# Three scatter blocks of 3, 3 and 2 chunks in the expert stage of a decoder trunk, the third one after the transposes

## The chip, the cores and the metric

One core of one Trainium2 chip runs the whole program. The metric is the device time of one execution in microseconds, lower is better; the time before is the median of three runs.

## The reference, cut to what matters

The reference is a two-layer decoder trunk over 512 tokens of width 1024. Each layer adds a mixer (a convolution in layer 0, a gated linear attention in layer 1), a cross-attention over 256 memory tokens, and a mixture of experts. The change lies in the mixture of experts, which picks two of 32 experts for every token:

```python
def hier_moe(h, w_grp, b_grp, w_exp, b_exp, w_gate, w_up, w_down):
...
    def expert_block(args):
        xb, e = args
        return (jax.nn.silu(xb @ w_gate[e]) * (xb @ w_up[e])) @ w_down[e]
...
    y = y_buf[dest] * g_flat[order][:, None].astype(h.dtype)
    out = jnp.zeros((T, D), h.dtype).at[token_idx].add(y)
```

Each expert has three matrices, of 1024x512, 1024x512 and 512x1024 float32, 2 MB each. They are read from memory once per layer, 12.58 MB for two experts.

## The kernel before, in words

The kernel is written engine by engine: one function for each engine, whose instructions run in the order in which they stand, with semaphores between them. The residual stream lies as `xT`, eight chunks of 128 features by 512 tokens. The experts of a layer are taken in 16 pairs (`p`, `NP = 16`), and two pairs make a quad (`q`). Nothing is indexed: tokens are gathered and scattered by products with one-hot matrices.

TensorE's list for pair `p` (`moe_segment` of the tensor block) is, before the change:

- `gates(p)` (L668), four small products with the gate table;
- `up(p, 0)` (L628), the gate matrices of both experts, 32 matmul records;
- `scatter(p, range(0, 4))` (L681), chunks 0 to 3 of the output of the pair before: for each chunk a product of `yhi` and one of `ylo` with `onehotT`, 512 columns, into one bank; then VectorE adds the bank to `xT` (`accumulate`, L1728);
- `up(p, 1)` (L628), the up matrices;
- `scatter(p, range(4, 8))`, chunks 4 to 7;
- `transposed(p)` (L688), four transposes of `hidden`, which VectorE makes (L1749) from the results of the two `up`; ScalarE copies them to `hidT` (L1324);
- one `gather` of two chunks for the next quad (L698), which ScalarE copies to `xg`; the last two pairs of a layer have none, since no quad is left;
- `down(p)` (L656), the down matrices, which need `hidT`; then ScalarE makes `yhi` (L1330) and VectorE `ylo` (L1755);
- a second `gather` (L698) and `one_hot_T(p)` (L707). The last pair of a layer has its down product in two halves (`down_half`, L642).

Gates, chunks, gathers and the one-hot transpose share three banks of PSUM (5, 6 and 7). `unit(r, p, k)` gives the place of each use in one sequence: `k` is 0 for the gates, 1 to 8 for the chunks 0 to 7, 9 and 10 for the gathers, 11 for the one-hot transpose. Use `n` goes to bank `n % 3`, and it waits until use `n - 3` has been read (`x_read0` to `x_read2`), by VectorE where that was a chunk, by ScalarE where it was a gather or the one-hot transpose. `x_full0` to `x_full2` say that a use has been written. `taken(p, k)` waits until a certain use has been read.

The weights come through SyncE's DMA queue into `ring`, six slots of 2 MB, exactly one pair. Each half slot (1 MB) is loaded again when the product that read it is done (`pair_loads`, L1049): the gate and up matrices by halves, the four halves of the down matrices together after `down`.

After the last pair `scatter(NP, range(0, C))` brings its eight chunks in one block.

Of the kernel before, what the change touches and what calls it, by code (L numbers as in the profile page):

```python
# [107 lines left out]
def build(nc, a, out):  # L108
# [3 lines left out]
    n = 0  # L112
# [9 lines left out]
    with ExitStack() as ctx:  # L122
# [111 lines left out]
        def bank(b, lo=0, hi=BANK):  # L234
            return PS[:, b * BANK + lo:b * BANK + hi]
# [104 lines left out]
        def unit(r, p, k):  # L340

            if p == -1:
                n = k - 8
            elif p == 0:
                n = 4 if k == 0 else k - 4
            elif p < NP - 2:
                n = 12 * p - 4 + k
            elif p == NP - 2:  # L350
                n = 12 * p - 4 + min(k, 9)
            else:
                n = 12 * p - 6 + min(k, 9) if p < NP else 12 * p - 9 + k
            return n % 3, PER_ROUND * r + n // 3
# [27 lines left out]
        def _(pe):  # L382
# [217 lines left out]
            def moe_segment(l, r):  # L600
# [3 lines left out]
                def use(p, k):  # L604
                    b, n = unit(r, p, k)
                    if not main or n:
                        pe.wait_ge(g[f"x_read{b}"], n)
                    return XBANK + b, g[f"x_full{b}"]

                def taken(p, k):  # L610
                    b, n = unit(r, p, k)
                    pe.wait_ge(g[f"x_read{b}"], n + 1)
# [59 lines left out]
                def scatter(p, cs):  # L672
                    if cs[0] == 0:
                        pe.wait_ge(g["ylo_done"], YS * r + p)
                        taken(p - 1, 11)
                    for c in cs:
                        if p == NP and c == C // 2:
                            pe.wait_ge(g["ylo_done"], YS * r + NP + 1)
                        b, done = use(p, 1 + c)
                        for w in (yhi, ylo):  # L680
                            mm = pe.matmul(bank(b), w[:, c * P:(c + 1) * P], onehotT[:, :],  # L681
                                           start=(w is yhi), stop=(w is ylo))
                        mm.then_inc(done, 1)
# [31 lines left out]
                for p in range(NP):  # L715
                    q, s = p // 2, p % 2
                    more = q + 1 < NQ
                    gates(p)
                    if s == 0:
                        for k in ((8, 9, 10, 11) if p == 0 else (9, 10)):  # L720
                            taken(p - 1, k)
                        if p >= 2:
                            for k in (9, 10):
                                taken(p - 2, k)
                    up(p, 0, "gate_full")
                    if p:
                        scatter(p, range(0, 4))
                    up(p, 1, "up_full")
                    if p:
                        scatter(p, range(4, 8))  # L730
                    transposed(p)
                    if more:
                        if s == 0:
                            pe.wait_ge(g["onehot_ready"], HOTS * r + q + 1 + TT)
                        gather(q + 1, p, 9, 4 * s)
                    if p < NP - 1:
                        down(p)
                        if more:
                            gather(q + 1, p, 10, 4 * s + 2)
                        one_hot_T(p)  # L740
                    else:
                        down_half(p, 0)
                        one_hot_T(p)
                        down_half(p, 1)
                    if main and p == NP // 2:
                        pe.wait_ge(cnt_ready, l + 1)
                        worst = pe.value_load(cnt_i[0:1, l:l + 1], min_val=0, max_val=T)
                    if main and p == NP - 3:
                        ahead = pe.mark_branch_hint_location()
# [766 lines left out]
        def _(dve):  # L1516
# [183 lines left out]
            def moe_segment(l, r):  # L1700
                g = seg[l]
                main = isinstance(r, int)

                def make_onehot(q):
                    n = 1 if q == 0 else TT
                    for t in range(0, TT, n):
                        tab = ptab[:, t:t + n, q * QUAD:(q + 1) * QUAD].unsqueeze(3).to_broadcast([P, n, QUAD, SL])
                        hot = onehot[:, q % 2, t:t + n, :].rearrange("p t (e s) -> p t e s", e=QUAD)
                        dve.tensor_tensor(hot, iota[:, :].unsqueeze(1).unsqueeze(1).to_broadcast([P, n, QUAD, SL]),
                                          tab, ALU.is_equal).then_inc(g["onehot_ready"], 1)  # L1710

                def take_gates(p):
                    b, n = unit(r, p, 0)
                    dve.wait_ge(g[f"x_full{b}"], n + 1)
                    col = (XBANK + b) * BANK
                    for half, dst, rows, done in ((0, gcol[0:SL, :], slice(0, SL), g["gates_in"]),
                                                  (2, rslot, slice(0, P), g["gates_ready"]),
                                                  (1, gcol[SL:, :], slice(SL, P), g[f"x_read{b}"])):
                        dve.tensor_reduce(dst, PS[rows, col + half:col + half + 4:3], AX.X, ALU.add).then_inc(done, 1)  # L1719
                    dve.wait_ge(g["gates_in"], NP * r + p + 1)  # L1720
                    dve.wait_ge(g["gates_ready"], NP * r + p + 1)
                    dve.wait_ge(g[f"x_read{b}"], n + 1)

                def accumulate(p, cs):
                    for c in cs:
                        b, n = unit(r, p, 1 + c)
                        dve.wait_ge(g[f"x_full{b}"], n + 1)
                        dve.tensor_tensor(xT[:, c, :], bank(XBANK + b), xT[:, c, :], ALU.add).then_inc(g[f"x_read{b}"], 1)  # L1728

                if not main:  # L1730
                    pf = ptab[:, :, :]
                    dve.tensor_scalar(pf, pf, -float(SL), None, ALU.add).then_inc(g["shifted"], 1)
                    dve.wait_ge(g["shifted"], r)
                make_onehot(0)
                if main:
                    router_gates(l)
                for p in range(NP):
                    q, s = p // 2, p % 2
                    if s == 0 and q + 1 < NQ:
                        if p:  # L1740
                            b, n = unit(r, p - 1, 11)
                            dve.wait_ge(g[f"x_full{b}"], n + 1)
                        make_onehot(q + 1)
                    take_gates(p)
                    if p:
                        accumulate(p, range(0, 4))
                    dve.wait_ge(g["silu_done"], NP * r + p + 1)
                    dve.wait_ge(g["up_full"], 2 * NP * r + (2 * p + 2))
                    dve.scalar_tensor_tensor(hidden, sil, gcol, bank(1), ALU.mult,  # L1749
                                             ALU.mult).then_inc(g["hidden_ready"], 1)  # L1750
                    if p:
                        accumulate(p, range(4, 8))
                    dve.wait_ge(g["yhi_done"], YS * r + p + 1)
                    n = 1024 if p < NP - 1 else 512
                    dve.tensor_tensor(ylo[:, 0:n], PS[:, 2 * BANK:2 * BANK + n], yhi[:, 0:n].bitcast(F32),  # L1755
                                      ALU.subtract).then_inc(g["ylo_done"], 1)
                    if main and p == NP // 2:
                        dve.wait_ge(cnt_ready, l + 1)
                        worst = dve.value_load(cnt_i[0:1, l:l + 1], min_val=0, max_val=T)
                        ahead = dve.mark_branch_hint_location()  # L1760
                accumulate(NP, range(0, 1))
                dve.wait_ge(g["yhi_done"], YS * r + NP + 1)
                dve.tensor_tensor(ylo[:, 512:1024], bank(3), yhi[:, 512:1024].bitcast(F32),
                                  ALU.subtract).then_inc(g["ylo_done"], 1)
                accumulate(NP, range(1, C))
                for b in range(3):
                    dve.wait_ge(g[f"x_read{b}"], PER_ROUND * r + PER_ROUND)
                return (worst, ahead) if main else None
# [267 lines left out]
```

## Time and profile before

| | |
|---|---|
| median of 3 runs | 1904.9 us (1904.06 to 1905.84) |
| the profiled execution's own time | 1904.18 us |
| its span | 1902.4 us |
| mean granted TensorE clock | 0.991 |
| TensorE busy | 1863.3 us, 98% of the span |
| VectorE busy | 586.9 us, 31% |
| ScalarE busy | 368.7 us, 19% |
| moved by DMA | 477.55 MB, mean 251 GB/s |
| share of the chain that ended last | TensorE 90%, VectorE 7% |

The span is the stretch from the first to the last instruction in one profiled execution; the time of a run holds a little more than that. "Busy" of TensorE is modelled from pipelined matmuls, so that 98% does not mean that every matmul runs at its shortest distance. The chain is the series of instructions, each released by the one before, that ends with the last instruction. PE is TensorE's matmul side, PEld its weight loads, DVE is VectorE, ACT ScalarE, SP SyncE.

### The profile page before, as it was taken

The numbers are of one execution on the slowest core, as the hardware profiler recorded it, in microseconds if no ns is written. First come the engines' busy times: TensorE is split into PE (matmuls) and PEld (weight loads), VectorE is DVE, ScalarE is ACT, GpSimd is POOL, SyncE is SP. The second block draws the span as 40 slices with busy tenths as digits, with TensorE's granted clock in tenths as the row PEclk, the third lists the DMA queues.
The fourth block names the chain that finished last, engine by engine and source line by source line (L and its number), as shares of the span: only waits on it lengthen the run. The fifth ranks groups of instructions, "written<-read, shape, count | busy, mean of one in ns | idle before, by whom it ended". The sixth has DMA issues, their size and how long they took to land.

```text
span 1902.4 us, 18477 instructions
## 1 busy us (share of the span) xinstructions
PE 1863.3 (98%) x7588; PEld 925.6 (49%) x7588; DVE 586.9 (31%) x1111; ACT 368.7 (19%) x623; POOL 160.7 (8%) x152
## 2 busy tenths in 40 slices
PE   8999999998999999999999999999999999999997
PEld 5445644545445454544444444455454444444443
DVE  3999211224122222221222322213322222222223
ACT  2433211212111110111124231122211111111112
POOL 0556110010000000000020000100100000000001
PEclk9999999998999999999999999999989999999998
DMA  9214422202999999999961211302169999999992
GB/s 361 97 40 164 160 89 89 83 10 105 413 405 406 412 405 415 403 415 404 371 226 44 89 44 45 132 1 92 55 262 415 403 412 408 414 405 414 405 413 117
DMA packets 90602, 477.55 MB, mean 251 GB/s; under 512 B 7759, under 2 KB 8189, under 8 KB 40973
## 3 DMA queue, kind: packets, MB, share of 16 engines
q1 hardware_dynamic: 89164, 470.88, 61.8%
q0 software_dynamic: 736, 3.15, 0.6%
q10 hardware_dynamic: 608, 2.24, 0.3%
q8 instruction: 62, 1.02, 0.2%
q14 instruction: 32, 0.25, 0.0%
HBM read 472.05 MB, written 4.19 MB: 250 GB/s over the span
## 4 chain that ended last, share of the span: by engine, by line
PE 90%; DVE 7%; issue 1%; DMA 1%; ACT 0%; POOL 0%; POOLq 0%; SPq 0%; DVEq 0%; ACTq 0%
PE PS L628 24%; PE PS L443 17%; PE PS L656 11%; PE PS L399 11%; PE PS L681 7%; PE PS L698 7%; DVE PS L1854 5%; PE PS L967 3%; PE PS L461 2%; PE PS L541 1%; PE PS L450 1%; PE PS L688 1%; PE PS L642 1%; PE PS L707 1%; PE PS L668 1%
## 5 line engine op out<-in xcount | busy, mean ns | idle before, releaser
L443 PE MATMUL PS<-hT,ring 128*128 128x512 f32 x640 | 277.7, 593 | 1.9 <-DVE xT L1728 1.2
L628 PE MATMUL PS<-ring,hT 128*64 128x512 f32 x1024 | 226.4, 595 | 1.3 <-DVE small L1719 1.3
L628 PE MATMUL PS<-ring,xg 128*64 128x512 f32 x1024 | 226.8, 595 | 0.0
L1728 DVE TENSOR_TENSOR xT<-PS,xT 128x512 f32<-128x512 f32 x256 | 158.6, 681 | 217.0 <-PE PS L681 217.0
L656 PE MATMUL PS<-ring,hT 128*64 128x512 f32 x960 | 212.6, 595 | 1.4 <-ACT hT L1324 1.4
L443 PEld LDWEIGHTS PS<-hT,ring 128*128 128x128 f32 x640 | 120.9, 190 | 149.9 <-issue 148.6
L628 PEld LDWEIGHTS PS<-ring,hT 128*64 128x64 f32 x1024 | 74.0, 137 | 132.8 <-issue 131.1
L628 PEld LDWEIGHTS PS<-ring,xg 128*64 128x64 f32 x1024 | 72.6, 137 | 132.2 <-issue 132.0
L1755 DVE TENSOR_TENSOR ylo<-PS,yhi 128x1024 fp32r<-128x1024 f32 (+1 forms) x32 | 38.1, 1191 | 294.1 <-ACT yhi L1330 285.1
L656 PEld LDWEIGHTS PS<-ring,hT 128*64 128x64 f32 x960 | 66.3, 137 | 125.4 <-issue 119.9
L681 PE MATMUL PS<-onehotT,yhi 128*128 128x512 f32 x256 | 114.9, 449 | 1.1 <-DVE xT L1728 1.1
L399 PE MATMUL PS<-ring,hT 128*128 128x512 f32 x256 | 111.8, 594 | 0.8 <-DVE RK L1895 0.8
L1854 DVE SCALAR_TENSOR_TENSOR PS<-RU,R,PS 128x512 f32<-128x512 f32 x168 | 111.3, 749 | 0.0
L681 PE MATMUL PS<-onehotT,ylo 128*128 128x512 f32 x256 | 101.2, 395 | 0.0
L1749 DVE SCALAR_TENSOR_TENSOR hT<-hT,small,PS 128x512 f32<-128x512 f32 x32 | 23.9, 747 | 212.5 <-PE PS L628 212.5
L698 PE MATMUL PS<-onehot,hhi 128*128 128x256 f32 x512 | 88.6, 296 | 0.0
L1324 ACT ACTIVATE hT<-PS 128x512 f32<-128x512 f32 x32 | 19.1, 598 | 355.7 <-PE PS L688 355.7
L681 PEld LDWEIGHTS PS<-onehotT,yhi 128*128 128x128 f32 x256 | 47.9, 187 | 82.5 <-issue 50.3
L443 PE MATMUL PS<-RC,ring 128*128 128x512 f32 x192 | 84.8, 595 | 0.0
L698 PE MATMUL PS<-onehot,hlo 128*128 128x256 f32 x512 | 83.4, 286 | 0.0
L698 PEld LDWEIGHTS PS<-onehot,hhi 128*128 128x128 f32 x512 | 71.5, 196 | 22.7 <-issue 22.7
L399 PEld LDWEIGHTS PS<-ring,hT 128*128 128x128 f32 x256 | 48.0, 190 | 59.3 <-issue 57.6
(282 smaller groups left out, 1746.6 us busy)
## 6 DMA issues: line engine op xcount, KB each, us to landing
ring<-in_moe_w_gate SPq DMA_DIRECT2D x128, 1024.0 KB, 11.2
ring<-in_moe_w_up SPq DMA_DIRECT2D x128, 1024.0 KB, 12.1
ring<-in_moe_w_down SPq DMA_DIRECT2D x128, 1024.0 KB, 9.2
ring<-in_xa_w_kv SPq DMA_DIRECT2D x16, 1024.0 KB, 7.4
ring<-in_gla_w_in SPq DMA_DIRECT2D x12, 1024.0 KB, 13.1
ring<-in_conv_w_in SPq DMA_DIRECT2D x8, 1024.0 KB, 14.8
ring<-in_xa_w_q SPq DMA_DIRECT2D x8, 1024.0 KB, 6.3
ring<-in_xa_w_o SPq DMA_DIRECT2D x8, 1024.0 KB, 6.8
```

Of the source, the lines that this page charges most:

```text
L399: mm = pe.matmul(o, lhs(k), rhs(k), start=(k == 0), stop=(k == nk - 1))
L443: mm = pe.matmul(bank(b), w[:, k * 512 + m * P:k * 512 + (m + 1) * P], src[:, k, :], start=(k == 0), stop=(k == C - 1))
L461: mm = pe.matmul(bank(b, (m % 2) * NMEM, (m % 2 + 1) * NMEM), w[:, k * 512 + m * P:k * 512 + (m + 1) * P], memT[:, k, :], start=(k == 0), ...
L628: mm = pe.matmul(PS[e * SL:(e + 1) * SL, kind * BANK:(kind + 1) * BANK], x[:, k, (2 * (p % 2) + e) * SL:(2 * (p % 2) + e + 1) * SL], ring[ ...
L656: mm = pe.matmul(PS[e * SL:(e + 1) * SL, (2 + half) * BANK:(3 + half) * BANK], hidT[:, k, e * SL:(e + 1) * SL], ring[:, pair_slot(l, 4 + e ...
L681: mm = pe.matmul(bank(b), w[:, c * P:(c + 1) * P], onehotT[:, :], start=(w is yhi), stop=(w is ylo))
L698: mm = pe.matmul(bank(b, (c - c0) * 256, (c - c0 + 1) * 256), h[:, t, c * P:(c + 1) * P], onehot[:, q % 2, t, :], start=(h is hhi and t == 0),
L967: mm = pe.matmul(bank(b), w[:, k * 512 + (m % 4) * P:k * 512 + (m % 4 + 1) * P], goT[k], start=(k == 0), stop=(k == C - 1))
L1728: dve.tensor_tensor(xT[:, c, :], bank(XBANK + b), xT[:, c, :], ALU.add).then_inc(g[f"x_read{b}"], 1)
L1749: dve.scalar_tensor_tensor(hidden, sil, gcol, bank(1), ALU.mult, ALU.mult).then_inc(g["hidden_ready"], 1)
L1755: dve.tensor_tensor(ylo[:, 0:n], PS[:, 2 * BANK:2 * BANK + n], yhi[:, 0:n].bitcast(F32), ALU.subtract).then_inc(g["ylo_done"], 1)
L1854: ins = dve.scalar_tensor_tensor(acc, src, w, acc, ALU.mult, ALU.add)
```

## The change

The eight chunks of a pair go in blocks of three, three and two. The third block stands between the transposes and `down`: behind the first gather where a pair has one, directly behind the transposes in the last two pairs of a layer. VectorE's list follows: three adds, then `hidden`, then five. In pairs with gathers the first gather now comes before chunks 6 and 7 in the sequence of uses, so `unit` gives `k = 9` the place 7 and the two chunks the places 8 and 9. `taken` loses waits on uses that lie earlier in the same bank than the one it keeps. The block of eight chunks behind the last pair is not touched, nor are the loads.

```diff
@@ -346,7 +346,7 @@
             elif p == 0:
                 n = 4 if k == 0 else k - 4
             elif p < NP - 2:
-                n = 12 * p - 4 + k
+                n = 12 * p - 4 + {7: 8, 8: 9, 9: 7}.get(k, k)
             elif p == NP - 2:
                 n = 12 * p - 4 + min(k, 9)
             else:
@@ -717,22 +717,21 @@
                     more = q + 1 < NQ
                     gates(p)
                     if s == 0:
-                        for k in ((8, 9, 10, 11) if p == 0 else (9, 10)):
+                        for k in ((8, 9, 10, 11) if p == 0 else (10,)):
                             taken(p - 1, k)
-                        if p >= 2:
-                            for k in (9, 10):
-                                taken(p - 2, k)
                     up(p, 0, "gate_full")
                     if p:
-                        scatter(p, range(0, 4))
+                        scatter(p, range(0, 3))
                     up(p, 1, "up_full")
                     if p:
-                        scatter(p, range(4, 8))
+                        scatter(p, range(3, 6))
                     transposed(p)
                     if more:
                         if s == 0:
                             pe.wait_ge(g["onehot_ready"], HOTS * r + q + 1 + TT)
                         gather(q + 1, p, 9, 4 * s)
+                    if p:
+                        scatter(p, range(6, 8))
                     if p < NP - 1:
                         down(p)
                         if more:
@@ -1743,13 +1742,13 @@
                         make_onehot(q + 1)
                     take_gates(p)
                     if p:
-                        accumulate(p, range(0, 4))
+                        accumulate(p, range(0, 3))
                     dve.wait_ge(g["silu_done"], NP * r + p + 1)
                     dve.wait_ge(g["up_full"], 2 * NP * r + (2 * p + 2))
                     dve.scalar_tensor_tensor(hidden, sil, gcol, bank(1), ALU.mult,
                                              ALU.mult).then_inc(g["hidden_ready"], 1)
                     if p:
-                        accumulate(p, range(4, 8))
+                        accumulate(p, range(3, 8))
                     dve.wait_ge(g["yhi_done"], YS * r + p + 1)
                     n = 1024 if p < NP - 1 else 512
                     dve.tensor_tensor(ylo[:, 0:n], PS[:, 2 * BANK:2 * BANK + n], yhi[:, 0:n].bitcast(F32),
```

How the instructions of the built programs stand, at three places. A row is a line, an operation, what it writes and reads, and the semaphores that it waits for.

TensorE, layer 0, a pair with gathers, from the last two chunks of the second block to the start of `down`, before:

```order
L681 MATMUL PS<-onehotT,yhi 128x512 [waits x_read0_0]
L681 MATMUL PS<-onehotT,ylo 128x512
L681 MATMUL PS<-onehotT,yhi 128x512 [waits x_read1_0]
L681 MATMUL PS<-onehotT,ylo 128x512
L688 MATMUL PS<-ident,hT 128x128 [waits hidden_ready_0]
L688 MATMUL PS<-ident,hT 128x128 x3
L698 MATMUL PS<-onehot,hhi 128x256 [waits x_read2_0,onehot_ready_0]
L698 MATMUL PS<-onehot,hhi 128x256 x3
L698 MATMUL PS<-onehot,hlo 128x256 x4
L698 MATMUL PS<-onehot,hhi 128x256 x4
L698 MATMUL PS<-onehot,hlo 128x256 x4
L656 MATMUL PS<-ring,hT 64x512 [waits ring_ld5_0,ring_ld4_0,hidT_ready_0]
```

The same stretch of the same pair now:

```order
L688 MATMUL PS<-ident,hT 128x128 [waits hidden_ready_0]
L688 MATMUL PS<-ident,hT 128x128 x3
L698 MATMUL PS<-onehot,hhi 128x256 [waits x_read0_0,onehot_ready_0]
L698 MATMUL PS<-onehot,hhi 128x256 x3
L698 MATMUL PS<-onehot,hlo 128x256 x4
L698 MATMUL PS<-onehot,hhi 128x256 x4
L698 MATMUL PS<-onehot,hlo 128x256 x4
L681 MATMUL PS<-onehotT,yhi 128x512 [waits x_read1_0]
L681 MATMUL PS<-onehotT,ylo 128x512
L681 MATMUL PS<-onehotT,yhi 128x512 [waits x_read2_0]
L681 MATMUL PS<-onehotT,ylo 128x512
L656 MATMUL PS<-ring,hT 64x512 [waits ring_ld5_0,ring_ld4_0,hidT_ready_0]
```

Two chunks went from ahead of the transposes to behind the gather, and the gather now waits for another bank, the one that the first chunk of the second block (chunk 3) was in.

TensorE, layer 0, the last pair, from the last chunk of the second block to the down product (L642), before and then now:

```order
L681 MATMUL PS<-onehotT,yhi 128x512 [waits x_read2_0]
L681 MATMUL PS<-onehotT,ylo 128x512
L688 MATMUL PS<-ident,hT 128x128 [waits hidden_ready_0]
L688 MATMUL PS<-ident,hT 128x128 x3
L642 MATMUL PS<-ring,hT 64x512 [waits ring_ld5_0,ring_ld4_0,hidT_ready_0]
```

```order
L688 MATMUL PS<-ident,hT 128x128 [waits hidden_ready_0]
L688 MATMUL PS<-ident,hT 128x128 x3
L681 MATMUL PS<-onehotT,yhi 128x512 [waits x_read1_0]
L681 MATMUL PS<-onehotT,ylo 128x512
L681 MATMUL PS<-onehotT,yhi 128x512 [waits x_read2_0]
L681 MATMUL PS<-onehotT,ylo 128x512
L642 MATMUL PS<-ring,hT 64x512 [waits ring_ld5_0,ring_ld4_0,hidT_ready_0]
```

Where nothing stood between the transposes and the product that needs their copy, two chunks stand now.

VectorE, layer 0, a pair with gathers, the adds (L1728) around `hidden` (L1749), before:

```order
L1728 TENSOR_TENSOR xT<-PS,xT 128x512 [waits x_full2_0]
L1728 TENSOR_TENSOR xT<-PS,xT 128x512 [waits x_full0_0]
L1749 SCALAR_TENSOR_TENSOR hT<-hT,small,PS 128x512 [waits up_full_0,silu_done_0]
L1728 TENSOR_TENSOR xT<-PS,xT 128x512 [waits x_full1_0]
L1728 TENSOR_TENSOR xT<-PS,xT 128x512 [waits x_full2_0]
L1728 TENSOR_TENSOR xT<-PS,xT 128x512 [waits x_full0_0]
```

And now, where the two lines have the numbers 1727 and 1748:

```order
L1727 TENSOR_TENSOR xT<-PS,xT 128x512 [waits x_full2_0]
L1748 SCALAR_TENSOR_TENSOR hT<-hT,small,PS 128x512 [waits up_full_0,silu_done_0]
L1727 TENSOR_TENSOR xT<-PS,xT 128x512 [waits x_full0_0]
L1727 TENSOR_TENSOR xT<-PS,xT 128x512 [waits x_full1_0]
L1727 TENSOR_TENSOR xT<-PS,xT 128x512 [waits x_full2_0]
L1727 TENSOR_TENSOR xT<-PS,xT 128x512 [waits x_full1_0]
```

The add of chunk 3 (bank `x_full0`) went behind `hidden`, and is the first of five.

## Rows read from the trace of the kernel before

**Rows 1.** The page, the chain that ended last, shares by engine

```profile
PE 90%; DVE 7%; issue 1%; DMA 1%; ACT 0%; POOL 0%; POOLq 0%; SPq 0%; DVEq 0%; ACTq 0%
```

**Rows 2.** One pair's stretch: its length, busy us (instructions) by engine, clock, DMA share, GB/s

```profile
618.20:649.03 30.83, 30.83 (x158) 14.70 (x157) 7.22 (x14) 4.00 (x6) 0.00 (x0) 1.00 1.00 409
```

**Rows 3.** Timeline of TensorE, first block: start, length, what (times in us)

```profile
626.10 0.50 PE L681 MATMUL PS<-onehotT,yhi 128*128 128x512 f32 x1
626.44 0.40 PE L681 MATMUL PS<-onehotT,ylo 128*128 128x512 f32 x1
...
627.38 0.39 PE L681 MATMUL PS<-onehotT,ylo 128*128 128x512 f32 x1
...
628.06 0.40 PE L681 MATMUL PS<-onehotT,ylo 128*128 128x512 f32 x1
628.38 7.09 PE L628 MATMUL PS<-ring,hT 128*64 128x512 f32 x32
```

**Rows 4.** Timelines of weight loads and VectorE, first block: [idle before <-releaser]

```profile
627.15 0.19 PEld L681 LDWEIGHTS PS<-onehotT,ylo 128*128 128x128 f32 x1
627.72 0.19 PEld L681 LDWEIGHTS PS<-onehotT,yhi 128*128 128x128 f32 x1 [0.38 <-DVE xT L1728]
...
626.98 2.48 DVE L1728 TENSOR_TENSOR xT<-PS,xT 128x512 f32<-128x512 f32 x4 [7.38 <-PE PS L681]
```

**Rows 5.** Timeline of TensorE, second block to the start of down

```profile
635.40 0.50 PE L681 MATMUL PS<-onehotT,yhi 128*128 128x512 f32 x1
...
636.67 0.40 PE L681 MATMUL PS<-onehotT,ylo 128*128 128x512 f32 x1
...
637.33 0.40 PE L681 MATMUL PS<-onehotT,ylo 128*128 128x512 f32 x1
637.57 0.63 PE L688 MATMUL PS<-ident,hT 128*128 128x128 f32 x4
637.96 0.72 PE L698 MATMUL PS<-onehot,hhi 128*128 128x256 f32 x4
...
640.03 7.09 PE L656 MATMUL PS<-ring,hT 128*64 128x512 f32 x32
```

**Rows 6.** Timeline of VectorE, second block

```profile
635.59 0.75 DVE L1749 SCALAR_TENSOR_TENSOR hT<-hT,small,PS 128x512 f32<-128x512 f32 x1 [6.13 <-PE PS L628]
636.25 2.48 DVE L1728 TENSOR_TENSOR xT<-PS,xT 128x512 f32<-128x512 f32 x4
```

**Rows 7.** Source line L681 over the whole trace: idle before it, us and times

```profile
  DVE xT L1728: 25.7, 70
```

**Rows 8.** Timeline of TensorE, end of the second gather of a pair

```profile
648.55 0.64 PE L698 MATMUL PS<-onehot,hlo 128*128 128x256 f32 x4
649.03 0.56 PE L707 MATMUL PS<-identR,onehot 128*128 128x128 f32 x4
```

**Rows 9.** Timeline of TensorE, layer 0, the last two pairs

```profile
912.92 0.50 PE L681 MATMUL PS<-onehotT,yhi 128*128 128x512 f32 x1
...
915.08 0.63 PE L688 MATMUL PS<-ident,hT 128*128 128x128 f32 x4
...
916.40 7.09 PE L656 MATMUL PS<-ring,hT 128*64 128x512 f32 x32 [0.69 <-ACT hT L1324]
...
944.22 3.65 PE L642 MATMUL PS<-ring,hT 128*64 128x512 f32 x16 [0.69 <-ACT hT L1324]
```

**Rows 10.** DMA of one pair (618.2 to 649), then of 650 to 660

```profile
DMA packets 1727, 12.59 MB, mean 409 GB/s; under 512 B 191, under 2 KB 191, under 8 KB 191
...
DMA packets 577, 4.21 MB, mean 421 GB/s; under 512 B 63, under 2 KB 63, under 8 KB 63
```

**Rows 11.** An up load's issue, L1049's time to landing, the up product that reads it

```profile
632.08 4.24 SPq L1049 DMA_DIRECT2D ring<-in_moe_w_up  x4
...
DMA to landing us min/median/max: 5.0/11.2/15.1
...
659.22 7.09 PE L628 MATMUL PS<-ring,xg 128*64 128x512 f32 x32
```

## The prediction

> **What bounds the kernel now.** I read the chain that ended last first: TensorE carries 90% of it [rows 1], so time is gained where TensorE's own series gets shorter, and hardly anywhere else. Then the table of busy time by stretch, cut at one expert pair: the pair takes 30.83 us, TensorE is busy for all of it at a granted clock of 1.00 (the 2.4 GHz level), VectorE for 7.22 us, ScalarE for 4.00, and the DMA engines are full as well, at 409 GB/s [rows 2]. So two things may bind in this stage, TensorE and the weight stream. The table of waits has none of TensorE's expert products behind a DMA, which speaks for TensorE. But a busy TensorE can still run at more than its shortest distance, and that shows only in the timeline, where the starts are to be subtracted.
>
> In the first block the matmuls of the scatter follow each other at 0.235 us (626.44 to 627.38 is four steps). The first step is 0.34 (626.10 to 626.44), 0.105 more. Between the sixth matmul (627.38) and the eighth (628.06) lie 0.68 us where two steps should take 0.47 [rows 3]. The weight loads say why: the load for the sixth matmul starts at 627.15, a step ahead of it; the next one only at 627.72, released by VectorE's add [rows 4]. There are three banks, and the fourth chunk needs that of the first. VectorE's adds begin at 626.98, and TensorE goes on at 627.72, 0.74 us later, which is one add and the signal. So a block of four chunks costs a wait of 0.105 us, and another 0.105 because the weight load behind a wait is not hidden. The second block shows the same: 636.67 to 637.33 is 0.66 for two steps [rows 5]. Over the whole trace the scatter has 70 weight loads or matmuls that wait for the add [rows 7]; 60 blocks (15 pairs, two blocks, two layers) account for most of them.
>
> **The change, part by part.** All durations are of the profiled execution.
>
> *First block, three chunks instead of four.* Before, from its first matmul to the up product: 626.10 to 628.38, 2.28 us. Now six matmuls, 1.28 us to the sixth, then the step into the product, which I take from 628.06 to 628.38 as 0.32: 1.60 us. Gain 0.68, of which 0.47 is work that only moves. Chunk 2 needs the bank of the gates, read before the block, so no wait takes the place of the old one.
>
> *Second block to down, a pair with gathers.* Before: 635.40 to 640.03, 4.63 us. Now six matmuls, 1.27 us to the sixth; the step into the transposes 0.24 (637.33 to 637.57); the transposes 0.39 (to 637.96); the gather up to its end 1.98, which is 2.07 (to 640.03) less 0.09 for the step into a product, the amount by which 0.32 exceeds 0.235; then four matmuls of the third block, three steps of 0.235 and 0.32 into the product. Sum 1.27 + 0.24 + 0.39 + 1.98 + 0.705 + 0.32 = 4.905, a cost of 0.275 [rows 5]. With the first block the pair gains 0.68 - 0.275 = 0.405 us.
>
> *Unknown: the step from the gather into the third block*, which has no row before. Upper bound 0.105, as from the product into the scatter [rows 3]. Lower bound 0, since no row has a step shorter than its matmul's distance: from the gather into the one-hot transpose, four matmuls of 256 columns take 0.48, which is 0.12 each, half of a 0.235 step and nothing on top [rows 8]. I take 0, since in both cases the operands keep one type and the full array. Ends for 26 pairs: 0 and 2.7 us.
>
> *Waits in the new place.* The transposes would start 1.51 us after the block's first matmul and need `hidden`; that ran from 635.59 for 0.75, ready at 0.94 [rows 5, 6]. The gather would start at 1.90 and needs the bank of chunk 3. Its add is VectorE's first behind `hidden`, starts at 636.25, and by the 0.74 of the first block the bank is free at 636.99, 1.59 after the block's start. Margin 0.31 us. Chunks 6 and 7 come 2 us later and need the banks of chunks 4 and 5, whose adds follow at 0.60 each. Four adds last 2.48 in all, so VectorE, idle for most of the pair [rows 2], has them done during down; `ylo` comes after that.
>
> *The last two pairs of a layer.* They have no gather there. From the second block to down: 912.92 to 916.40, 3.48 us, of which TensorE stood idle for 0.69 behind ScalarE's copy; the last pair shows the same 0.69 [rows 9]. Down cannot start sooner than 1.32 after the transposes (915.08 to 916.40). Now: 1.51 to the transposes, 0.39 through them, then the third block behind float32 work, a first step of 0.34, two of 0.235 and 0.32 out, together 1.13. Sum 3.03. From the transposes to down that is 1.52, more than 1.32, so the copy is covered. Gain 0.45, with the first block's 0.68 this is 1.13 us. Bank waits: chunk 6 starts at 1.90, chunk 3's bank is free at 1.59; chunk 7 starts at 2.48, chunk 4's bank is free at 2.19.
>
> *The `taken` waits and `unit`* only remove waits on uses that a later use of the same bank implies, and rename places; nothing. SyncE's loads wait on the same three products as before; VectorE and ScalarE have the same work.
>
> *Sum.* Pairs 1 to 13 of two layers: 26 x 0.405 = 10.5 us. Pairs 14 and 15: 4 x 1.13 = 4.5 us. Pair 0 has no scatter and the eight chunks at the end keep their waits. Together 15.0 us. Against the profiled execution's 1904.18 this gives 1889.2; the median is 0.7 higher, 1904.9, so 1889.9 for the median of the changed kernel.
>
> *Cover of the weights.* A shorter pair needs a faster stream. In the middle of a pair it runs at 421 GB/s, and one pair's 12.59 MB take 29.9 us at that rate [rows 10]. The new period is 30.83 - 0.405 = 30.4 us. It fits, with half a microsecond left. If it did not fit, there is a reserve: the up load is issued from 632.08 to 636.3, lands at most 15.1 us later, by 651.4, and is read from 659.22 on [rows 11]. That is 7.8 us, while TensorE would run ahead of a stream that got no faster by 13 x 0.405 = 5.3 us in a layer.
>
> **The rivals.** *The steps cost more.* The stall goes, but each entry into the third block costs 0.105, and the step out of it or a short wait for the bank takes another 0.05: 26 x 0.155 = 4.0 us less gain, 1893.9. For it: TensorE pays such a step wherever float32 products and the scatter meet. Against it: the row behind the gather [rows 8].
>
> *The weight stream binds.* DMA share 1.00 [rows 2] speaks for it. If the stream set the pace at 30.83 us per pair, TensorE would wait for weights what it saved, and the time would stay at 1904.9. Against it: 421 against 409 GB/s and the reserve above [rows 10, 11]. The Trainium skill, HBM Reference, section Specifications, gives an effective 358 GB/s per core, which would make 35.2 us per pair an estimate for the stream and this change worth nothing. The trace does not agree, with 409 GB/s over a whole pair; the page itself says that a core streaming alone measures well above its share, about 425.
>
> *Slower: the gather waits for VectorE.* Before, the fourth chunk stood behind the first add of its block; now the gather, and with it ScalarE's copy and down, could. If the bank were free only after all three adds of the second block, at 636.99 + 1.20 = 638.19, the gather, wanted at 637.30, would lose 0.89 and 0.105 for the weight load, 0.995 in all. Then a pair is 0.59 longer: 26 x 0.59 = 15.3, less the last pairs' 4.5, and the time is 1915.7. With the last pairs' gain this turns the sign from 0.47 us of waiting per pair (26 x (0.47 + 0.105 - 0.405) = 4.4), that is with a bank free 0.78 us later than the row says. Against it: use 12p + 3 waits for use 12p, chunk 3, and VectorE has it first behind `hidden`.
>
> **How the numbers follow.** A measurement of this kernel can tell about 0.2%, 3.8 us, from no change. Forecast 1889.9, chance 0.80, its own range 1888 to 1893 (the sum, the 2.7 us of the unknown step, and 1 to 2 us for the spread of runs and for differences read to 0.01 us and taken 52 times). Costlier steps, 0.11, up to 1895.5: still over 0.2% faster. Stream binds, 0.05, within 0.2%. Gather waits, 0.04, slower. So faster 0.91, same 0.05, slower 0.04. The range is 1888.0 to 1895.5.
>
> **What would show it.** The cut of one pair should be 30.4 us long, and in the first block 1.60 us should lie between the first matmul and the up product. The waits of weight loads on the add should fall from 70 to the 10 that the 60 blocks leave over, those of the eight chunks at the end. The transposes should start 1.51 us after the second block's first matmul and the gather 0.39 later, without an idle time behind VectorE. The 0.69 behind ScalarE's copy should be gone in the last two pairs. In the cut of a pair the DMA should show about 414 GB/s. The prediction is wrong if TensorE shows a wait on a DMA, if the gather's weight load waits for the add, or if the pair is longer than 30.7 us.

## The result, and the profile after

| | before | changed |
|---|---|---|
| median | 1905.19 us (1904.06 to 1905.84, 4 runs) | 1890.33 us (1889.81 to 1891.35, 4 runs) |
| the profiled execution's own time | 1904.18 us | 1891.35 us |
| its span | 1902.4 us | 1889.3 us |
| mean granted TensorE clock | 0.991 | 0.991 |

The ratio is 0.9923, with a 95% interval of 0.9911 to 0.9936. The kernel is 14.9 us faster, where 15.0 was forecast, and the median of 1890.33 lies 0.4 us above the predicted 1889.9. The medians alone can't tell the gain that closely: by the interval it lies between 12.2 and 17.0 us.

The cut of one pair in the changed kernel, from the start of its second gather to that of the next pair's, answers to [rows 2]. Columns: the stretch, its length, busy us (instructions) of TensorE, its weight loads, VectorE, ScalarE and GpSimd, then granted clock, DMA share and GB/s:

```profile
615.71:646.14 30.43, 30.43 (x159) 14.73 (x157) 7.32 (x13) 4.00 (x6) 0.00 (x0) 1.00 1.01 414
```

0.40 us less than before at the same clock, and the stream goes at 414 GB/s instead of 409, as it must. "Busy" says 100% in both, so the 0.40 us are not to be found in that column, only in the starts. The timeline of TensorE, first block and then second block to down, answers to [rows 3] and [rows 5] (start, length, what):

```profile
625.61 0.50 PE L681 MATMUL PS<-onehotT,yhi 128*128 128x512 f32 x1
...
626.89 0.39 PE L681 MATMUL PS<-onehotT,ylo 128*128 128x512 f32 x1
627.21 7.09 PE L628 MATMUL PS<-ring,hT 128*64 128x512 f32 x32
634.23 0.50 PE L681 MATMUL PS<-onehotT,yhi 128*128 128x512 f32 x1
...
635.49 0.40 PE L681 MATMUL PS<-onehotT,ylo 128*128 128x512 f32 x1
635.73 0.63 PE L688 MATMUL PS<-ident,hT 128*128 128x128 f32 x4
636.11 0.72 PE L698 MATMUL PS<-onehot,hhi 128*128 128x256 f32 x4
636.67 0.64 PE L698 MATMUL PS<-onehot,hlo 128*128 128x256 f32 x4
...
637.62 0.64 PE L698 MATMUL PS<-onehot,hlo 128*128 128x256 f32 x4
638.10 0.40 PE L681 MATMUL PS<-onehotT,yhi 128*128 128x512 f32 x1
638.33 0.40 PE L681 MATMUL PS<-onehotT,ylo 128*128 128x512 f32 x1
...
639.12 7.09 PE L656 MATMUL PS<-ring,hT 128*64 128x512 f32 x32
```

A step is the distance between the starts of two instructions that follow each other on TensorE. The first block takes 1.60 us, the second to down 4.89, and no step in either waits for an add. The unknown step, from the gather into the third block, is free: the last four matmuls of the gather take 0.48 (637.62 to 638.10), and the first step of the block is 0.23, not 0.34.

Line L681 over the whole trace, idle before it, answers to [rows 7]:

```profile
  DVE xT L1727: 3.4, 10
```

The 60 waits of the 60 blocks are gone; the 10 of the two final blocks of eight are left. The last two pairs of layer 0 answer to [rows 9]:

```profile
908.32 0.50 PE L681 MATMUL PS<-onehotT,yhi 128*128 128x512 f32 x1
...
909.82 0.63 PE L688 MATMUL PS<-ident,hT 128*128 128x128 f32 x4
910.21 0.48 PE L681 MATMUL PS<-onehotT,yhi 128*128 128x512 f32 x1
...
910.52 0.40 PE L681 MATMUL PS<-onehotT,ylo 128*128 128x512 f32 x1
...
911.30 7.09 PE L656 MATMUL PS<-ring,hT 128*64 128x512 f32 x32
```

Down starts 1.48 us after the transposes with no idle time before it, against 1.32 with 0.69 idle. The profiled spans differ by 13.1 us, less than the medians. From the first transposes of layer 0 to the last (483.26 to 942.89 before, 484.39 to 936.44 now) the gain is 7.58 us, and in layer 1 (1410.80 to 1870.41, now 1404.86 to 1856.84) 7.63; 0.16 a layer goes back behind the last transposes, where two chunks now stand. That is 14.9 us. The code ahead of the experts, which the change does not touch, was 1.1 us later in this execution (e7 and e10 below, two executions of one kernel, differ there by 1.0), and the code between and behind the experts of the two layers 0.7.

### The profile page after: what moved, and what is told of

Read it like the earlier page. It is cut to its first block, busy times and chain, and to the rows that moved or that the text cites. A ratio compares the mean times of both kernels' runs of the same rounds, so it can differ in the third digit from the quotient of the medians.

```text
span 1889.3 us, 18449 instructions
## 1 busy us (share of the span) xinstructions
PE 1852.9 (98%) x7588; PEld 924.3 (49%) x7588; DVE 589.7 (31%) x1111; ACT 368.7 (20%) x623; POOL 160.8 (9%) x152
## 4 chain that ended last, share of the span: by engine, by line
PE 91%; DVE 7%; issue 1%; DMA 1%; POOL 0%; ACT 0%; POOLq 0%; SPq 0%; DVEq 0%; ACTq 0%
PE PS L628 24%; PE PS L443 17%; PE PS L656 11%; PE PS L399 11%; PE PS L698 7%; PE PS L681 7%; DVE PS L1853 5%; PE PS L966 3%; PE PS L461 2%; PE PS L541 1%; PE PS L450 1%; PE PS L688 1%; PE PS L642 1%; PE PS L707 1%; PE PS L668 1%
## 5 line engine op out<-in xcount | busy, mean ns | idle before, releaser
L628 PE MATMUL PS<-ring,hT 128*64 128x512 f32 x1024 | 226.3, 595 | 1.3 <-DVE small L1718 1.3
L628 PE MATMUL PS<-ring,xg 128*64 128x512 f32 x1024 | 226.8, 595 | 0.0
L656 PE MATMUL PS<-ring,hT 128*64 128x512 f32 x960 | 212.6, 595 | 0.0
L628 PEld LDWEIGHTS PS<-ring,hT 128*64 128x64 f32 x1024 | 72.7, 137 | 134.0 <-issue 132.3
L628 PEld LDWEIGHTS PS<-ring,xg 128*64 128x64 f32 x1024 | 70.7, 137 | 133.9 <-issue 133.7
L656 PEld LDWEIGHTS PS<-ring,hT 128*64 128x64 f32 x960 | 66.3, 137 | 130.3 <-issue 129.4
L681 PE MATMUL PS<-onehotT,yhi 128*128 128x512 f32 x256 | 108.7, 425 | 1.1 <-DVE xT L1727 1.1
L681 PE MATMUL PS<-onehotT,ylo 128*128 128x512 f32 x256 | 101.4, 396 | 0.0
L681 PEld LDWEIGHTS PS<-onehotT,yhi 128*128 128x128 f32 x256 | 48.1, 188 | 61.4 <-issue 50.3
## 6 DMA issues: line engine op xcount, KB each, us to landing
ring<-in_moe_w_up SPq DMA_DIRECT2D x128, 1024.0 KB, 13.1
ring<-in_conv_w_in SPq DMA_DIRECT2D x8, 1024.0 KB, 14.9
```

The lines of the kernel that those rows point to most:

```text
L628: mm = pe.matmul(PS[e * SL:(e + 1) * SL, kind * BANK:(kind + 1) * BANK], x[:, k, (2 * (p % 2) + e) * SL:(2 * (p % 2) + e + 1) * SL], ring[ ...
L656: mm = pe.matmul(PS[e * SL:(e + 1) * SL, (2 + half) * BANK:(3 + half) * BANK], hidT[:, k, e * SL:(e + 1) * SL], ring[:, pair_slot(l, 4 + e ...
```

## The experiments

Three questions come first: do the two kinds of pair bring what the sum says, is it the bank wait and not the shorter block, and was the way it could have ended slower priced rightly. Then where the next bound lies.

**e1, the pairs with gathers alone.** The last two pairs keep 4 and 4:

```diff
-                        scatter(p, range(0, 3))
+                        scatter(p, range(0, 3 if p < NP - 2 else 4))
...
-                        scatter(p, range(3, 6))
+                        scatter(p, range(3, 6) if p < NP - 2 else range(4, 8))
...
-                    if p:
+                    if 0 < p < NP - 2:
                         scatter(p, range(6, 8))
```

(VectorE's list likewise.)

> Blocks of 3, 3 and 2 in pairs 1 to 13 alone; the last two pairs of a layer keep 4 and 4. My theory (a stall of the fourth chunk and the weight load behind it, 0.405 us per pair): 26 x 0.405 = 10.5 us under the kernel before, ratio 0.9945, the pair 30.43 us long. Rival (the gain comes mostly from ScalarE's copy that is covered in the last pairs): under 3 us, ratio over 0.998.

Measured: 1894.88 us, ratio 0.9942 (0.9928 to 0.9955), 11.0 us under the kernel before (1905.85 in the same runs). The transposes of successive pairs with gathers lie 30.43 or 30.44 us apart, but for one pair in each layer (see the last section).

**e2, the last two pairs alone.** The same edit with the condition turned round, and the old order of uses.

> Blocks of 3, 3 and 2 in pairs 14 and 15 alone; pairs 1 to 13 keep 4 and 4. My theory: 4 x 1.13 = 4.5 us under the kernel before, ratio 0.9976, and no idle time of 0.69 us behind ScalarE's copy. Rival (the copy is covered but the two chunks cost as much where they stand now): within 1 us of the kernel before, ratio 0.9995 to 1.0005. The two parts should add up to the whole change.

Measured: 1901.59 us, ratio 0.9978 (0.9969 to 0.9987), 4.3 us under. The pairs with gathers are 30.83 to 30.85 us apart. In the table of waits ScalarE's copy no longer stands before L656 and L642. The two parts add up: 11.0 + 4.3 = 15.3 us for 14.9. Both rivals fall.

**e3, the gather waits for all three adds.** The case that I had priced as slower:

```diff
                             pe.wait_ge(g["onehot_ready"], HOTS * r + q + 1 + TT)
+                        if p:
+                            taken(p, 6)
                         gather(q + 1, p, 9, 4 * s)
```

> The changed kernel, but the first gather of pairs 1 to 13 waits until VectorE has added all three chunks of the second block, as in the rival that ended slower. If TensorE's order is all that binds: the gather starts 0.9 us later and its weight load shows 0.105 more, 1.0 us per pair, 26 us over the changed kernel (some 1916 us). If VectorE were slack (the adds done by the time of the gather): no difference, 1890. If something behind the gather had room (ScalarE's copy of the transposes, the weights), less than 26 us: a part of the wait is made up for.

Measured: 1914.13 us, ratio 1.0044 (1.0028 to 1.0059), 23.8 us over the changed kernel's 1890.33, or some 23 if each is taken against the kernel before in its own runs (8.3 over it and 14.9 under it). The timeline of TensorE, from the transposes on (in brackets the idle time before, and who ended it):

```profile
639.22 0.63 PE L688 MATMUL PS<-ident,hT 128*128 128x128 f32 x4
640.51 0.74 PE L698 MATMUL PS<-onehot,hhi 128*128 128x256 f32 x4 [0.66 <-DVE xT L1729]
641.08 0.64 PE L698 MATMUL PS<-onehot,hlo 128*128 128x256 f32 x4
```

The gather starts 1.29 us behind the transposes instead of 0.38, 0.91 later, and most pairs are 31.33 to 31.38 us apart, 0.93 more. Nothing behind the gather made up for it, 26 x 0.93 being 24.2: TensorE's order is what binds. The 0.105 that I added for a weight load behind a wait does not show, because the gather's first four matmuls take 0.56 us behind the float32 transposes anyway (636.11 to 636.67 in the changed kernel) and 0.57 here. So the place where the chunks were put had to be one that the bank's order frees in time.

**e4, gathers without their low part.** The gathers leave out the products with `hlo`, so that the tokens reach the experts with their high part alone:

```diff
-                        for h in (hhi, hlo):
+                        for h in (hhi,):
```

> The changed kernel, whose gathers leave out the products with the low part of the tokens (hlo): 16 matmuls of 0.119 us less in each pair with gathers, 1.9 us. TensorE alone would need 28.5 us per pair. My theory (the stream can give 421 GB/s, 29.9 us per pair, with a reserve of 8 us or more): the first pairs of a layer at 28.5 us, the later ones at 29.9 us with TensorE's products waiting for a DMA, and the DMA without a gap. Rival (the stream was already at its limit in the changed kernel, 30.4 us per pair): the later pairs at 30.4 us.

Measured: 1859.35 us. Layer 0 has seven distances between transposes of 27.69 to 28.52 us, then one of 28.91, one of 30.84, and the rest 29.78 to 30.08. TensorE's waits in the stretch of layer 0 (engine, line, released by: us in total, times, longest), and the stream in the stretch 800 to 840:

```profile
PE PS L628 <- DMA ring<-in_moe_w_up: 7.9, 8, 1.1
PE PS L628 <- DMA ring<-in_moe_w_gate: 2.2, 3, 1.3
PE PS L642 <- DMA ring<-in_moe_w_down: 1.6, 1, 1.6
...
DMA packets 2310, 16.84 MB, mean 421 GB/s; under 512 B 257, under 2 KB 257, under 8 KB 257
```

Both sides of the cover are seen: the reserve lasts for about seven pairs, then the stream sets the pace at some 29.9 us and 421 GB/s. The changed kernel, at 30.43, has 0.5 us per pair left above that.

**e5, blocks of three and five, both before the transposes.** The uses have the order of the kernel before again; VectorE's list is that of the changed kernel.

```diff
-                        scatter(p, range(3, 6))
+                        scatter(p, range(3, 8))
                     transposed(p)
...
-                    if p:
-                        scatter(p, range(6, 8))
```

> Two blocks, of three chunks and of five, both ahead of the transposes; no third block. My theory (three banks, an add of 0.60 us per chunk against 0.47 us of matmuls): the first block gains 0.68 us, but in the second chunk 6 waits for chunk 3's add (0.05 and 0.105 for the weight load) and chunk 7 comes as fast as the adds allow, so that the transposes start some 2.8 us after the block's first matmul; the pair gains 0.05 to 0.2 us of the 0.405, 1 to 5 us in all, 1901 to 1904. Rival (what counts is that the first block is short, and the place of the third doesn't matter): the pair 30.43 us as in the changed kernel.

Measured: 1904.66 us against 1905.68, ratio 0.9994 (0.9985 to 1.0003), no difference that can be told, and 0.7 us above the upper end that I expected (the last section has what one pair of each layer adds). The timeline of TensorE, second block:

```profile
604.62 0.50 PE L681 MATMUL PS<-onehotT,yhi 128*128 128x512 f32 x1
...
605.88 0.40 PE L681 MATMUL PS<-onehotT,ylo 128*128 128x512 f32 x1
606.21 0.50 PE L681 MATMUL PS<-onehotT,yhi 128*128 128x512 f32 x1
606.54 0.40 PE L681 MATMUL PS<-onehotT,ylo 128*128 128x512 f32 x1
606.81 0.50 PE L681 MATMUL PS<-onehotT,yhi 128*128 128x512 f32 x1
...
607.38 0.63 PE L688 MATMUL PS<-ident,hT 128*128 128x128 f32 x4
```

The first block is as short as in the changed kernel, and it helps nothing: steps of 0.33 and 0.27 before the fourth and the fifth chunk, each followed by one of 0.33. The transposes start 2.76 us after the block (2.8 forecast), and a pair takes 30.75 instead of 30.84. It is the third block's place, with the gather's 1.98 us in which VectorE catches up, that brings the 0.40.

**e6, no block between the gate and the up product.** For pairs 1 to 13 chunks 0 to 2 stand before the transposes, chunks 3 to 7 behind the gather (VectorE's list likewise):

```diff
-                n = 12 * p - 4 + {7: 8, 8: 9, 9: 7}.get(k, k)
+                n = 12 * p - 4 + {4: 5, 5: 6, 6: 7, 7: 8, 8: 9, 9: 4}.get(k, k)
...
-                    if p:
+                    if p >= NP - 2:
                         scatter(p, range(0, 3))
...
-                        scatter(p, range(3, 6))
+                        scatter(p, range(3, 6) if p >= NP - 2 else range(0, 3))
...
-                        scatter(p, range(6, 8))
+                        scatter(p, range(6 if p >= NP - 2 else 3, 8))
```

> Pairs 1 to 13: no block between the gate and up products; three chunks ahead of the transposes, five behind the gather. One step into and one out of float32 products fall away, 0.105 + 0.09 = 0.19 us per pair. If the five chunks behind the gather ran without a wait: the pair 30.24 us, 5 us under the changed kernel. I expect chunk 7 to wait for chunk 4's add (0.09 and 0.105), which takes the gain back: the pair 30.35 to 30.5 us, 1889 to 1892.

Measured: 1888.04 us, ratio 0.9908 (0.9892 to 0.9923), 2.0 us under e8, the changed kernel on the same chip; a pair takes 30.35 us. The pair is at the lower end of what I expected, the time 1.0 us below it, and the sum behind both is not what happened. The timeline of TensorE, the block of five, then the next pair's two products and the block behind them:

```profile
606.00 0.40 PE L681 MATMUL PS<-onehotT,yhi 128*128 128x512 f32 x1
...
608.35 0.39 PE L681 MATMUL PS<-onehotT,ylo 128*128 128x512 f32 x1
...
618.58 13.95 PE L628 MATMUL PS<-ring,hT 128*64 128x512 f32 x64
632.46 0.50 PE L681 MATMUL PS<-onehotT,yhi 128*128 128x512 f32 x1
```

The block's nine steps take 2.35 us where 9 x 0.235 is 2.12: the waits for banks, with the weight loads behind them, cost 0.24, more than the 0.19 that was to be saved. What pays for them is a term that the sum didn't have. With nothing between them the two products take 13.88 us (618.58 to 632.46), where in the changed kernel each takes 7.02 (627.21 to 634.23), 14.04 together, so that some 0.15 us more is saved. 0.19 + 0.15 - 0.24 is the 0.09 to 0.10 by which the pair is shorter.

**e7, the first block ahead of the gates; e8, the changed kernel beside it.** In pairs 1 to 14:

```diff
+                    if 0 < p < NP - 1:
+                        scatter(p, range(0, 3))
                     gates(p)
...
                         down(p)
+                        one_hot_T(p)
                         if more:
                             gather(q + 1, p, 10, 4 * s + 2)
-                        one_hot_T(p)
```

(ScalarE's copies and VectorE's adds in the same order, `unit` from a list of the uses, VectorE makes the next quad's one-hot behind the gates.)

> Pairs 1 to 14: the first block of three goes ahead of the gates, behind the second gather of the pair before, so that it has work of its own type on both sides; the one-hot transpose and its copy go ahead of that gather, so that they are ready. Steps saved: 0.105 in and 0.09 out, 0.19 us per pair, 28 x 0.19 = 5.3 us under the changed kernel, 1885, the pair 30.24 us. Rival: the block now needs ylo 0.04 us after VectorE has it, and its banks sooner; a wait of 0.2 us or more there takes the gain back (1890 or more). Second rival: the weight stream, at 29.9 us per pair, begins to bind; then TensorE's table of waits shows a DMA.

> The changed kernel again, on the chip of the three others: 1890 to 1891, ratio 0.992 to 0.9925, the pair 30.44 us.

Measured: e7 1887.66 us, ratio 0.9907 (0.9892 to 0.9922), a pair 30.30 us; e8 1890.04 us, ratio 0.9922 (0.9909 to 0.9936), 30.44. So e7 gains 2.4 us on the changed kernel, between the 5.3 of my theory and the nothing of the first rival. No expert product stands behind a DMA in TensorE's waits. Of the two steps that were to be saved, the one at the block's entry is not; timelines of TensorE, of its weight loads and of VectorE:

```profile
616.99 0.64 PE L702 MATMUL PS<-onehot,hlo 128*128 128x256 f32 x4
617.47 0.50 PE L685 MATMUL PS<-onehotT,yhi 128*128 128x512 f32 x1
617.81 0.39 PE L685 MATMUL PS<-onehotT,ylo 128*128 128x512 f32 x1
...
617.47 0.19 PEld L685 LDWEIGHTS PS<-onehotT,yhi 128*128 128x128 f32 x1
...
616.19 1.23 DVE L1762 TENSOR_TENSOR ylo<-PS,yhi 128x1024 fp32r<-128x1024 f32 x1 [7.26 <-ACT yhi L1335]
```

The matmul starts on time, 0.48 behind the gather's last four, but `ylo` is there only at 617.42, so its weight load begins with it, and not 0.11 before. The first step is 0.34. The block with the step out of it takes 1.51 us (617.47 to 618.98, where the gates start) instead of 1.60, so 0.09 of the 0.19 is there. The rest of the pair's 0.14 was not in my sum: the two products side by side save 0.15 as in e6 (619.52 to 633.40), while the one-hot transpose right behind down takes 0.50 instead of 0.40, the gates 0.54 instead of 0.48, and the gather's first four matmuls 0.53 instead of 0.58.

**e9, with `ylo` in two halves; e10, e7 again beside it.** The block's three chunks need only the first half:

```diff
+                    if p < NP - 2:
+                        dve.tensor_tensor(ylo[:, 0:512], bank(2), yhi[:, 0:512].bitcast(F32),
+                                          ALU.subtract).then_inc(g["ylo_done"], 1)
+                        dve.tensor_tensor(ylo[:, 512:1024], bank(3), yhi[:, 512:1024].bitcast(F32),
+                                          ALU.subtract).then_inc(g["ylo_done"], 1)
```

(The first block waits for the first of the two signals, the second block for the other.)

> The kernel with the first block ahead of the gates, and VectorE makes ylo in two halves of 512 columns for pairs 0 to 13; the first block (chunks 0 to 2) needs only the first half, 0.55 us sooner. My theory (in that kernel the block's first weight load waits 0.05 us for ylo, and this costs 0.105 more because the load is not hidden): the first step falls from 0.34 to 0.235 and the 28 waits of the gates for an add go too, the pair 30.17 to 30.20 us, 3 to 4 us less, some 1884. Rival (a first step of 0.34 belongs to every block of the scatter that starts with yhi, wait or no wait): the pair stays at 30.30 us.

> The kernel with the first block ahead of the gates again, on the same chip as the one with ylo in halves: 1887 to 1888, the pair 30.30 us.

Measured: e9 1883.12 us, ratio 0.9886 (0.987 to 0.9903), a pair 30.19 to 30.21 us; e10 1886.34 us, ratio 0.9904 (0.9888 to 0.9921), 30.30. The same place in e9:

```profile
615.59 0.64 PE L705 MATMUL PS<-onehot,hlo 128*128 128x256 f32 x4
616.07 0.40 PE L688 MATMUL PS<-onehotT,yhi 128*128 128x512 f32 x1
616.30 0.40 PE L688 MATMUL PS<-onehotT,ylo 128*128 128x512 f32 x1
...
615.95 0.19 PEld L688 LDWEIGHTS PS<-onehotT,yhi 128*128 128x128 f32 x1
...
614.79 0.69 DVE L1766 TENSOR_TENSOR ylo<-PS,yhi 128x512 fp32r<-128x512 f32 x1 [7.26 <-ACT yhi L1338]
```

The load is 0.12 ahead of its matmul and the first step 0.23. The rival (0.34 belongs to every first step) falls. The time came out near the 1884 and the pair at the upper end of 30.17 to 30.20, 3.2 us less than e10, of which 28 x 0.105 = 2.9 is the first step. The other half of my theory fails: the gates' wait for an add did not go. The weight loads of e9 still show it, 7.5 us in 28 times, where e10 has 8.1:

```profile
PEld PS L673 <- DVE xT L1736: 7.5, 28, 0.3
```

This kernel leaves out no work and is 22.0 us faster than the kernel before (1905.11 in its runs).

## Why the prediction was right

- *What bounds.* TensorE's own series did: what was taken out of it came off the time in e1, e2, e6, e7 and e9, and what was put in (e3) came on top, 23 to 24 us for 26 x 0.93 = 24.2.
- *First block, 1.60 us.* Measured 1.60.
- *Second block to down, 4.905 us.* Measured 4.89. With the first block this is 0.42 for the 0.405 read at one pair; the distance of the transposes gives 0.40 (30.83 to 30.43).
- *The unknown step.* Taken as 0 between 0 and 0.105; it is 0. The rival of costlier steps falls with it.
- *`hidden` and the transposes.* The prediction had `hidden` ready 0.57 us before the transposes and let it cost nothing. It is 0.56 (634.42 + 0.75 to 635.73), where the kernel before had 1.23, and it costs nothing in all pairs with a scatter but two, which lose 0.24 us together (last section).
- *The gather's bank.* Free in time by the forecast's 0.31 us. The changed trace has the adds from 635.08, and by the 0.74 of [rows 4] the bank is free at 635.82, for a gather at 636.11: 0.29.
- *Last two pairs, 3.03 us.* Measured 2.98, since the first step behind the transposes is 0.31 (910.21 to 910.52) and not the 0.34 that I took from behind a product. Their 4.5 us came as 4.3 in e2.
- *Cover of the weights.* It holds, with the DMA at the 414 GB/s that was named, and e4 measured the floor at 29.9 us, the figure worked out from 421 GB/s.
- *The rival that ends slower.* Its mechanism and its sign are right (1914.1 for 1915.7), its size was 1.0 us per pair and is 0.93. The step that failed is the 0.105 for the weight load, which adds nothing where the step is long already.

What the range allowed on top, up to 1895.5, was for steps that cost more, and was not needed. The gain is about four times the 0.2% that can be told from no change. That the medians meet the forecast to 0.1 us is in part luck, since their interval is 12.2 to 17.0 us; what bears the sum out is the trace, with 0.40 us per pair, and e1 and e2, which measured its two parts apart.

## What to carry to other kernels

When an engine shows 100% busy, subtract the starts of its instructions: a ring of three banks made every fourth chunk wait 0.1 us and cost another 0.1 for a weight load that could no longer be hidden, 60 times. A block should be no longer than the ring, and what remains goes behind other work that gives the reading engine time to catch up; shortening one block and lengthening the next (e5) moves the wait, it does not remove it. Weigh this against the steps between kinds of work: e6 has a block of five and pays 0.24 us of waits for it, and is still 2.0 us faster than the changed kernel, since by the trace its steps and its two products side by side save 0.34. Before an operand is used by a block that follows at once, have it ready one weight load sooner than the matmul needs it (e7 against e9).

## What the runs showed of the hardware

- A weight load that is late by 0.11 us costs 0.105 us of TensorE, though the matmul itself starts on time: e7 against e9, 30.30 to 30.20 us per pair. Behind the float32 products of L628 the first step is 0.34 in every block shown, with the weight load starting together with its matmul there too; behind the transposes it is 0.31.
- Two expert products with nothing between them take 13.88 us, and two with a block of the scatter between them 2 x 7.02 = 14.04, from first matmul to what follows (e6, e7 and e9 against the changed kernel).
- In the changed kernel one pair of each layer is longer than the others, 30.59 us in layer 0 and 30.52 in layer 1: the gather follows its transposes after 0.56 us (layer 1: 0.45) instead of 0.39. The trace shows what is late. VectorE starts `hidden` 0.37 us later than in the other pairs with a scatter, 0.56 behind the second block's first matmul instead of 0.19, though the product that it waits for is not late. It is ready at 726.85, and the transposes' first weight load starts 0.14 ahead of its matmul instead of 0.23:

```profile
634.42 0.75 DVE L1748 SCALAR_TENSOR_TENSOR hT<-hT,small,PS 128x512 f32<-128x512 f32 x1 [6.04 <-PE PS L628]
...
726.10 0.75 DVE L1748 SCALAR_TENSOR_TENSOR hT<-hT,small,PS 128x512 f32<-128x512 f32 x1 [6.41 <-PE PS L628]
726.90 0.58 PEld L688 LDWEIGHTS PS<-ident,hT 128*128 128x128 f32 x4
...
727.04 0.63 PE L688 MATMUL PS<-ident,hT 128*128 128x128 f32 x4
727.60 0.71 PE L698 MATMUL PS<-onehot,hhi 128*128 128x256 f32 x4
```

  The same two `hidden` (pair 8 of layer 0, pair 5 of layer 1) are late by the same 0.35 to 0.37 us in e1, e3, e4, e5 and e8. In e5 the transposes come later and have room for it, but the adds behind `hidden` are late too, and chunks 6 and 7 wait for them ahead of the transposes: the two pairs that end there take 31.12 and 31.10 us instead of 30.75, 0.7 us together. In the kernel before and in e2, e6, e7, e9 and e10 no pair shows it. Why VectorE starts late there was not tested and stays open.
